# Four pieces instead of five for a far block's copy, and layer 1's key gather moved ahead of layer 0's value stores

## The chip, the cores and the metric

The kernel runs on one core of one Trainium2 chip. The metric is the device time of one execution in microseconds (us); the median of three runs of the kernel before is 405.74 us (405.36 to 406.79).

## The reference, cut to what matters

A trunk of two layers is run for a prompt (256 positions) and for 8 samples with one new position each. A layer normalises x, multiplies it with one combined input matrix, runs three groups side by side (a causal convolution of width 31, trailing means, and a dilated attention), and multiplies the concatenated results with an output matrix. What matters here are the samples' caches of keys and values, 2048 positions of 6 heads of 64 per sample and layer:

```python
kk = jnp.concatenate([k_buf, k], axis=1)
vv = jnp.concatenate([v_buf, v], axis=1)
o = dilated_attention(q, kk, vv, k_buf.shape[1])
yc = o.reshape(B, T, C_ATT) * jax.nn.silu(c_gate)
n_keep = min(MAX_WINDOW, kk.shape[1])
new_k = kk[:, -n_keep:]
new_v = vv[:, -n_keep:]
y = jnp.einsum('bte,ed->btd', jnp.concatenate([ya, yb, yc], axis=-1), w_out)
```

So each cache (2 layers, keys and values, 8 samples, 2048 rows of 1536 B) comes out once more, shifted by one row, and the attention of a sample reads only a part of its rows: the last 128 (near), every 4th of the 384 before them (mid), and every 16th of the first 1536 (far).

## The kernel before, in words

All arithmetic is float32, 128 partitions wide. TensorE (PE) carries the projections: 25 tiles of input weights per layer (`proj`, L586, 8 matmuls of 128x264 each) and 8 of output weights (`wout`, L723). Weights come in loads of three tiles (1536 KB) through a ring of three buffers `wt`; ScalarE (ACT) issues the next load when it has taken a buffer's last tile (`load_behind`). VectorE (DVE) runs the convolution's taps and the samples' scores. The order of all of this is one hand-written list, `SCHEDULE`, which every compute engine walks. Neither the list nor any instruction of PE, DVE or ACT is touched by the change.

The caches are moved in two ways.

- **The copies (GpSimd, POOL, L504).** Rows that the attention does not read go straight from the input cache to the output in DRAM. `COPIES` lists 48 transfers per layer: for keys and values and each of 8 samples two far halves (48 blocks of 16 rows, of which 15 are copied) and one mid part (96 blocks of 4 rows, of which 3 are copied). `max_dma_last_dim` caps a piece at `PIECE_ROWS` = 3 rows, 4608 B. So a far block is five pieces and a mid block one. POOL issues all 96 transfers in a row, layer 1's first, and waits for nothing but room in its queue.
- **The rows that are read (SyncE, SP).** `gather` loads near, mid and far rows into `kt` (keys) or `vt` (values), 20 slots per partition, 8 transfers for each of the three spans; `put_back` (L411, L416) stores the same tile into the output, shifted by one row. `kt` and `vt` are single buffers, so a layer's gather waits until the layer before has been read and stored.

SP issues all of these in one stream of program order, with waits on semaphores in between. Per layer: gather keys, gather values, store keys, states (the small state loads of the next layer and state copies of this one), store values. PE needs a layer's gathered values at step `spv` (L657), where it waits for all 24 transfers at once:

```python
pe.wait_ge(S["v_in"], nth(l, "v_in", per["v_in"]))
for j in range(a, b):
    v = vt[:, j, :] if j < NEW else kvb[:, 1, :]
    nc.tensor.matmul(psc[0:NH * NS, 0:C_ATT], spm[...], v, start=(j == 0), stop=(j == SLOTS))
```

DVE needs the keys at `sscore` (L1081), span by span. A value gather of layer 1 waits, span by span, until the stores of that span of layer 0 have landed (`v_near_out`, `v_mid_out`, `v_far_out`); a key gather does so with `k_near_out` and so on. At the end, ACT and DVE copy the turned output into `y_tok` (the memory of `kt`), SP issues its five stores (L477 to L485), and waits for everything.

Of the kernel before, what the change touches and what calls it, by code (L numbers as in the profile page):

```python
# [26 lines left out]
DEPTH, D_MODEL, SEQ, NS, PAST = 2, 1024, 256, 8, 2048  # L27
C_CONV, C_POOL, C_ATT, HD = 384, 256, 384, 64
# [17 lines left out]
GATHER = []  # L46
# [119 lines left out]
assert set(TABLE_BEFORE) <= set(SCHEDULE)  # L166
ACT_SCHEDULE = [_s for _s in SCHEDULE if _s != "ln2"]
ACT_SCHEDULE.insert(ACT_SCHEDULE.index(("proj", PIDX[("b_gate", 0)])), "ln2")
PIECE_ROWS = 3
GATHER_ROWS = 2  # L170
COPIES = [(kind, s, a, b, d) for kind in "kv" for s in range(NS) for a, b, d in
          ((0, GATHER[1][0] // 2, GATHER[2][1]), (GATHER[1][0] // 2, GATHER[1][0], GATHER[2][1]),
# [1 line left out]
SPANS = ("near", "mid", "far")  # L174
IN_FLIGHT = 16
# [4 lines left out]
def sample_rows(s):  # L180

    first = 2 * PER_S * (s // 2) + s % 2
    return slice(first, first + 2 * PER_S - 1, 2)
# [67 lines left out]
def trunk_program(nc, ins, const, const_at, outs):  # L251
    (y_prompt, y_sample, o_conv_p, o_pool_p, o_k_p, o_v_p, o_conv_s, o_pool_s, o_k_s, o_v_s) = outs
    with ExitStack() as ctx:
# [6 lines left out]
        def sem(name):  # L260
            return ctx.enter_context(nc.semaphore(name))
# [76 lines left out]
        per = {}  # L338

        S = {}  # L340
# [23 lines left out]
        copy_out = [sem(f"copy_out{i}") for i in range(IN_FLIGHT)]  # L364
# [11 lines left out]
        def nth(l, name, n):  # L376

            return l * per[name] + n + first.get(name, 0)
# [8 lines left out]
        def _(sp):  # L387
            def one(name, l):
                return ins[name][bass.ds(l, 1)]

            def gather(kind, l, g, name):

                tile = {"k": kt, "v": vt}[kind]
                (lo, d, n), at = GATHER[g], SPAN_AT[g]
                for s in SAMPLE_ORDER:
                    rows = one(f"cache_{kind}_win", l)[:, s, lo:lo + d * n * PER_S]
                    rows = rows.rearrange("o (a b e) h d -> (o a) b e (h d)", a=PER_S, e=d)[:, :, 0, :]
                    sp.dma_start(tile[sample_rows(s), at:at + n, :], rows, max_dma_last_dim=GATHER_ROWS * C_ATT * 4).then_inc(S[name], 16)  # L398

            def put_back(kind, l, g):  # L400

                name = f"{kind}_{SPANS[g]}_out"
                tile = {"k": kt, "v": vt}[kind]
                out = {"k": o_k_s, "v": o_v_s}[kind][bass.ds(l, 1)]
                (lo, d, n), at = GATHER[g], SPAN_AT[g]
                skip = 1 if lo == 0 else 0
                for s in SAMPLE_ORDER:
                    r = sample_rows(s)
                    rows = out[:, s, lo - 1 + d * n * skip:lo - 1 + d * n * PER_S]
                    rows = rows.rearrange("o (a b e) h d -> (o a) b e (h d)", b=n, e=d)[:, :, 0, :]  # L410
                    sp.dma_start(rows, tile[r.start + 2 * skip:r.stop:2, at:at + n, :]).then_inc(S[name], 16)  # L411
                if skip:
                    for r in range(2):
                        rows = out[:, r:NS:2, d - 1:d * n - 1]
                        rows = rows.rearrange("o s (b e) h d -> (o s) b e (h d)", e=d)[:, :, 0, :]
                        sp.dma_start(rows, tile[r:P:2 * PER_S, at + 1:at + n, :]).then_inc(S[name], 16)  # L416

            def states(l):
                if l > 0:
                    sp.wait_ge(S["tr_full"], nth(l - 1, "tr_full", TR["st1"] + 1))  # L420
                sp.dma_start(st_conv[:, :, :], one("state_conv", l).rearrange("o (r s) w c -> (o s w) r c", r=2)
                             ).then_inc(S["st_in"], 16)
                sp.dma_start(st_pool[:, :], one("state_pool", l).rearrange("o s w c -> (o s w) c")).then_inc(S["st_in"], 16)  # L423

            def keep_states(l):
                for name, out, keep in (("state_conv", o_conv_s, TAIL - 1), ("state_pool", o_pool_s, POOL_BUF - 1)):
                    sp.dma_start(out[bass.ds(l, 1), :, 0:keep].rearrange("o s w c -> (o s) (w c)").rearrange("s (e x) -> e s x", e=16),  # L427
                                 one(name, l)[:, :, 1:keep + 1].rearrange("o s w c -> (o s) (w c)").rearrange("s (e x) -> e s x", e=16))\
                        .then_inc(S["state_out"], 16)
# [8 lines left out]
            sp.dma_start(cst[:, early:], const[:, early:]).then_inc(const_in, 16)  # L438
            states(0)

            for l in range(DEPTH):
                if l == 0:
                    sp.wait_ge(S["pj_full"], nth(l, "pj_full", PIDX[("a_glu", 0)] + 1))
                if l > 0:
                    sp.wait_ge(S["ks_used"], nth(l - 1, "ks_used", len(SCORE_CUTS)))
                for g, span in enumerate(SPANS):
                    if l > 0:
                        sp.wait_ge(S[f"k_{span}_out"], nth(l - 1, f"k_{span}_out", per[f"k_{span}_out"]))
                    gather("k", l, g, f"k_{span}_in")

                if l == 0:
                    sp.wait_ge(x_copied, XROUNDS)
                    sp.wait_ge(S["pj_full"], nth(l, "pj_full", PIDX[("k", AT - 1)] + 1))
                else:
                    sp.wait_ge(S["sc_full"], nth(l - 1, "sc_full", NH + 1))
                for g, span in enumerate(SPANS):
                    if l > 0:
                        sp.wait_ge(S[f"v_{span}_out"], nth(l - 1, f"v_{span}_out", per[f"v_{span}_out"]))
                    gather("v", l, g, "v_in")

                if l == DEPTH - 1:
                    sp.wait_ge(S["pj_full"], nth(l, "pj_full", PIDX[("c_gate", AT - 1)] + 1))
                for g, span in enumerate(SPANS):
                    sp.wait_ge(S[f"k_{span}_in"], nth(l, f"k_{span}_in", per[f"k_{span}_in"]))
                    put_back("k", l, g)
                if l < DEPTH - 1:
                    states(l + 1)
                keep_states(l)

                if l == DEPTH - 1:  # L470
                    sp.wait_ge(S["sc_full"], nth(l, "sc_full", NH + 1))
                sp.wait_ge(S["v_in"], nth(l, "v_in", per["v_in"]))
                for g in range(len(SPANS)):
                    put_back("v", l, g)
# [17 lines left out]
        @block.gpsimd  # L492
        def _(pool):
            for name in START:
                pool.sem_inc(S[name], 1)

            pool.wait_ge(x_in, 32)
            for l in reversed(range(DEPTH)):
                for i, (kind, s, a, b, d) in enumerate(COPIES):
                    n = (DEPTH - 1 - l) * len(COPIES) + i  # L500
                    cache, out = (ins["cache_k_win"], o_k_s) if kind == "k" else (ins["cache_v_win"], o_v_s)
                    dst = out[l, s, a:b].rearrange("(c e f) h d -> c e (f h d)", c=16, f=d)[:, :, 0:(d - 1) * C_ATT]
                    src = cache[l, s, a:b].rearrange("(c e f) h d -> c e (f h d)", c=16, f=d)[:, :, C_ATT:d * C_ATT]
                    pool.dma_start(dst, src, max_dma_last_dim=PIECE_ROWS * C_ATT * 4).then_inc(copy_out[n % IN_FLIGHT], 16)  # L504

        @block.tensor
        def _(pe):
# [234 lines left out]
        def _(act):  # L742
# [18 lines left out]
            for l in range(DEPTH):  # L761
# [13 lines left out]
                for step in ACT_SCHEDULE:  # L775
# [121 lines left out]
                    elif kind in ("conv_p", "conv_s", "pool_ps"):  # L897
# [5 lines left out]
                        for dst, src, _, _ in copies:  # L903
                            last = A(dst[:, :], src, ACT.Copy, scale=0.5 if kind in ("conv_p", "conv_s") else 1.0)
                        last.then_inc(S["tr_free"], 1)
                        act.wait_ge(S["tr_free"], nth(l, "tr_free", TR[step] + 1))
                        for dst, _, out, row in copies:
                            o = out[bass.ds(l, 1)].rearrange("l b w c -> (l b w) c") if row is None else \
                                out[bass.ds(l, 1), :, row].rearrange("l s c -> (l s) c")
                            act.dma_start(o, dst[:, :]).then_inc(S["tail_out"], 16)  # L910
# [338 lines left out]
```

## Time and profile before

| what | value |
|---|---|
| median of 3 runs | 405.74 us |
| the profiled execution's own time | 407.23 us |
| its span, first to last instruction | 405.4 us |
| PE busy | 342.6 us (85%) |
| DVE busy | 231.9 us (57%) |
| DMA, moved over the span | 158.20 MB, mean 390 GB/s |
| DMA packets | 50,569 |
| mean granted clock of PE | 0.952 |

How to read it: a row of the profile's groups names line, engine, operation, tiles and count. "SPq", "ACTq" and "POOLq" are the engines as issuers of transfers; the queues that carry them are q1 for SP, q10 for ACT and q0 for POOL. A queue's row gives its packets, their bytes, and the time that they took as a share of 16 DMA engines over the stretch. A packet of 4 B closes a transfer on each engine and counts as a packet. A bracket behind a timeline row gives the idle time before it and what ended it.

### The profile page before, as it was taken

What the parts mean: (1) busy time and instruction counts of PE and PEld (TensorE: products, weight loads), DVE (VectorE), ACT (ScalarE), POOL (GpSimd) and SP (SyncE); (2) the same over time, 40 slices, a digit from 0 to 9 for tenths busy, and PEclk for the clock granted to TensorE, in tenths of its full rate; (3) what the DMA queues carried; (4) which work ended last, traced back from release to release, by engine and by line L of the source; (5) the groups of instructions that cost most, each with busy time, mean ns of one, the idle gap of its engine ahead of it and who ended that gap; (6) DMA issues with size and microseconds to landing.
All of it is one profiled execution on the core that took longest, in us unless ns stands there. A gap on an engine that the chain in (4) does not pass through costs nothing.

```text
span 405.4 us, 4582 instructions
## 1 busy us (share of the span) xinstructions
PE 342.6 (85%) x1534; PEld 265.4 (65%) x1534; DVE 231.9 (57%) x518; ACT 99.3 (24%) x234; POOL 56.5 (14%) x100
## 2 busy tenths in 40 slices
PE   3899999974899699899799999972989699899900
PEld 2688888852677465788588888852667555588800
DVE  2526998898769744310425898897857973311100
ACT  3201144311623423010200225321434324101010
POOL 3802022020220202202022020210201202000000
PEclk9999999997899999999899999998699999999965
DMA  8999999999999999999999999999999999999993
GB/s 291 415 419 415 417 415 411 413 385 404 409 386 399 415 360 365 416 365 417 418 412 395 418 418 414 416 410 417 405 389 373 415 391 338 411 391 386 349 374 154
DMA packets 50569, 158.20 MB, mean 390 GB/s; under 512 B 5400, under 2 KB 19938, under 8 KB 50034
## 3 DMA queue, kind: packets, MB, share of 16 engines
q0 software_dynamic: 19968, 84.94, 53.2%
q1 hardware_dynamic: 20812, 38.16, 25.6%
q10 hardware_dynamic: 9766, 34.82, 21.4%
q8 instruction: 12, 0.20, 0.2%
q14 instruction: 11, 0.09, 0.1%
HBM read 139.35 MB, written 104.42 MB: 601 GB/s over the span
## 4 chain that ended last, share of the span: by engine, by line
SPq 53%; PE 29%; DMA 8%; issue 2%; ACT 1%; DVE 1%; ACTq 0%; DVEq 0%
SPq L398 29%; SPq L411 20%; PE pj L586 15%; DMA vt<-in_cache_v_win 7%; PE pj L723 7%; PE psc L657 3%; SPq L427 2%; DMA vt<-in_x_sample 1%; SPq L423 1%; PE ptr L509 1%; SPq L416 1%; ACT hT L753 1%; PE prt L598 0%; PE ps L596 0%; PE ps L707 0%
## 5 line engine op out<-in xcount | busy, mean ns | idle before, releaser
L586 PE MATMUL pj<-hT,wt 128*128 128x264 f32 x800 | 191.2, 397 | 3.4 <-DVE hT L996 3.4
L586 PEld LDWEIGHTS pj<-hT,wt 128*128 128x128 f32 x800 | 154.5, 196 | 33.6 <-issue 7.3
L1141 DVE SCALAR_TENSOR_TENSOR yc<-u_ext,cst,yc 128x256 f32<-128x256 f32 x180 | 76.2, 480 | 2.8 <-DVE u_smp L1024 0.6
L723 PE MATMUL pj<-mix,wt 128*128 128x264 f32 x256 | 59.5, 387 | 0.0
L723 PEld LDWEIGHTS pj<-mix,wt 128*128 128x128 f32 x256 | 48.0, 190 | 8.0
L504 POOL DMA_DIRECT2D out<-in_cache_v_win x48 | 28.1, 591 | 162.5 <-issue 162.5
L504 POOL DMA_DIRECT2D out<-in_cache_k_win x48 | 28.2, 594 | 130.8 <-issue 124.2
L1211 DVE TENSOR_TENSOR xT<-xT,pj 128x264 f32<-128x264 f32 x16 | 6.9, 429 | 53.2 <-PE pj L723 53.2
L657 PE MATMUL psc<-vt,spm 128*48 128x384 f32 x80 | 26.9, 488 | 0.7 <-DMA vt<-in_cache_v_win 0.7
L822 ACT ACTIVATE ex<-pj 128x264 f32<-128x264 f32 x22 | 8.6, 391 | 76.8 <-PE pj L586 62.4
L509 PE MATMUL ptr<-cst,sc 128*128 128x128 f32 x36 | 7.1, 310 | 17.8 <-DVE sc L1057 17.8
L657 PEld LDWEIGHTS psc<-vt,spm 128*48 128x48 f32 x80 | 9.4, 123 | 15.5 <-issue 15.4
L1081 DVE TENSOR_TENSOR tok<-kt,qb 128x1536 f32<-128x1536 f32 x10 | 17.6, 1758 | 3.0 <-DMA kt<-in_cache_k_win 2.4
L509 PEld LDWEIGHTS ptr<-cst,sc 128*128 128x128 f32 x36 | 4.4, 153 | 21.6 <-DVE sc L1057 21.2
L1031 DVE SCALAR_TENSOR_TENSOR mix<-ex,pj 128x264 f32<-128x264 f32 x16 | 6.9, 428 | 19.9 <-ACT ex L822 19.6
L1084 DVE TENSOR_REDUCE ssc<-tok 128x24 f32<-128x1536 f32 x10 | 17.5, 1753 | 0.3
L1022 DVE SCALAR_TENSOR_TENSOR u_ext<-ex,pj 128x256 f32<-128x256 f32 x6 | 2.5, 422 | 23.4 <-ACT ex L822 23.4
L778 ACT ACT_TABLE_LOAD x12 | 15.4, 1283 | 0.4
L929 ACT ACTIVATE hT<-xT 128x264 f32<-128x264 f32 x8 | 3.4, 422 | 33.2 <-DVE xT L1211 33.2
L805 ACT ACTIVATE sqg<-pj 128x264 f32<-128x264 f32 x12 | 4.7, 392 | 26.9 <-PE pj L586 24.2
L881 ACT ACTIVATE sc<-sc,nmax 128x128 f32<-128x128 f32 x12 | 4.8, 402 | 25.0 <-DVE nmax L1050 19.4
L624 PE MATMUL psc<-qk 64*128 64x128 f32 x24 | 6.4, 352 | 5.1 <-DVE qk L1011 5.1
(165 smaller groups left out, 314.2 us busy)
## 6 DMA issues: line engine op xcount, KB each, us to landing
out<-in_cache_k_win POOLq DMA_DIRECT2D x32, 1080.0 KB, 70.1
out<-in_cache_v_win POOLq DMA_DIRECT2D x32, 1080.0 KB, 68.3
wt<-in_w ACTq DMA_DIRECT2D x21, 1536.0 KB, 14.8
out<-in_cache_k_win POOLq DMA_DIRECT2D x16, 432.0 KB, 66.6
out<-in_cache_v_win POOLq DMA_DIRECT2D x16, 432.0 KB, 69.5
kt<-in_cache_k_win SPq DMA_DIRECT2D x32, 144.0 KB, 25.3
vt<-in_cache_v_win SPq DMA_DIRECT2D x32, 144.0 KB, 22.7
kt<-in_cache_k_win SPq DMA_DIRECT2D x16, 192.0 KB, 17.1
```

Source lines behind the costliest of these rows:

```text
L398: sp.dma_start(tile[sample_rows(s), at:at + n, :], rows, max_dma_last_dim=GATHER_ROWS * C_ATT * 4).then_inc(S[name], 16)
L411: sp.dma_start(rows, tile[r.start + 2 * skip:r.stop:2, at:at + n, :]).then_inc(S[name], 16)
L504: pool.dma_start(dst, src, max_dma_last_dim=PIECE_ROWS * C_ATT * 4).then_inc(copy_out[n % IN_FLIGHT], 16)
L509: return nc.tensor.transpose(out, in_, C["ident"][0:rows, 0:rows])
L586: last = nc.tensor.matmul(pj[n % RING][:, 0:T], w[:, k * P:(k + 1) * P], hT[:, k, :], start=(k == 0), stop=(k == KD - 1))
L657: nc.tensor.matmul(psc[0:NH * NS, 0:C_ATT], spm[:, j * NH:(j + 1) * NH, :].rearrange("p h s -> p (h s)"), v, start=(j == 0), stop=(j == SL ...
L723: last = nc.tensor.matmul(pj[n % RING][:, 0:T], w[:, k * P:(k + 1) * P], mix[:, k, :], start=(k == 0), stop=(k == KD - 1))
L778: nc.scalar.preload_act_table_set(TABLE_BEFORE[step])
L822: A(ex[:, e % 2, :], src, ACT.Tanh, scale=0.5).then_inc(S["sig_ok"], 1)
L1081: V.tensor_tensor(tok4[:, :, :], kt[:, a:b, :], qb[:, None, :].to_broadcast([P, b - a, C_ATT]), ALU.mult).then_inc(S["kprod_ok"], 1)
L1084: last = V.tensor_reduce(ssc[:, a:b, :], tok4[:, :, :].rearrange("p j (h d) -> p j h d", h=NH), AX.X, ALU.add)
L1141: last = V.scalar_tensor_tensor(out=yc[:, t, 0:SEQ], in0=x_w, scalar=par[:, ROW_CW + w * CT + t:ROW_CW + w * CT + t + 1], in1=yc[:, t, 0:S ...
```

## The change

`PIECE_ROWS` gives way to `PIECES = 4`: the cap on a piece becomes 15 rows / 4 = 5760 B (3.75 rows). A far block's 23040 B go in four pieces instead of five; a mid block's 4608 B stay one piece. On SP, the gather of layer 1's keys is issued behind layer 0's state copies and ahead of layer 0's value stores, where it was behind them. No transfer is added or removed.

```diff
-PIECE_ROWS = 3
+PIECES = 4
...
-            for l in range(DEPTH):
+            def gather_keys(l):
                 if l == 0:
                     sp.wait_ge(S["pj_full"], nth(l, "pj_full", PIDX[("a_glu", 0)] + 1))
                 if l > 0:
...
+            gather_keys(0)
+            for l in range(DEPTH):
                 if l == 0:
                     sp.wait_ge(x_copied, XROUNDS)
                     sp.wait_ge(S["pj_full"], nth(l, "pj_full", PIDX[("k", AT - 1)] + 1))
                 else:
                     sp.wait_ge(S["sc_full"], nth(l - 1, "sc_full", NH + 1))
...
                 if l < DEPTH - 1:
                     states(l + 1)
                 keep_states(l)
+                if l < DEPTH - 1:
+                    gather_keys(l + 1)
 
                 if l == DEPTH - 1:
                     sp.wait_ge(S["sc_full"], nth(l, "sc_full", NH + 1))
...
-                    pool.dma_start(dst, src, max_dma_last_dim=PIECE_ROWS * C_ATT * 4).then_inc(copy_out[n % IN_FLIGHT], 16)
+                    pool.dma_start(dst, src, max_dma_last_dim=(GATHER[2][1] - 1) * C_ATT * 4 // PIECES).then_inc(copy_out[n % IN_FLIGHT], 16)
```

SP's stream between the two layers, as a difference (+ is the kernel after; names are destination<-source, `vt` and `kt` the tiles, "x8" eight transfers in a row):

```order
 L427 DMA out<-in_state_conv 16x8x696
 L427 DMA out<-in_state_pool 16x8x224
+L398 DMA kt<-in_cache_k_win 16x4x768 x8
+L398 DMA kt<-in_cache_k_win 16x6x384 x16
 L411 DMA out<-vt 16x3072 x8
 L411 DMA out<-vt 96x1x384 x8
 L411 DMA out<-vt 90x1x384 x8
 L416 DMA out<-vt 4x5x384 x2
-L398 DMA kt<-in_cache_k_win 16x4x768 x8
-L398 DMA kt<-in_cache_k_win 16x6x384 x16
 L398 DMA vt<-in_cache_v_win 16x4x768 x8
 L398 DMA vt<-in_cache_v_win 16x6x384 x16
```

The 24 key loads and the 26 value stores have changed places; the 24 value loads of layer 1 stand behind the same transfers as before.

POOL's stream at its start, before:

```order
L504 DMA out<-in_cache_k_win 48x5x1152 x2
L504 DMA out<-in_cache_k_win 96x1152
```

and after the change:

```order
L516 DMA out<-in_cache_k_win 48x4x1440 x2
L516 DMA out<-in_cache_k_win 96x1152
```

The two far halves go from 48 x 5 pieces of 1152 elements to 48 x 4 pieces of 1440; the mid part is as it was. This pattern repeats for all 32 pairs of halves.

## Rows read from the trace of the kernel before

**Rows 1.** The page's first line: the span.
```profile
span 405.4 us, 4582 instructions
```

**Rows 2.** The page's table of DMA queues over the whole span.
```profile
q0 software_dynamic: 19968, 84.94, 53.2%
q1 hardware_dynamic: 20812, 38.16, 25.6%
q10 hardware_dynamic: 9766, 34.82, 21.4%
```

**Rows 3.** Windows: busy us (x instructions) per engine, granted clock, DMA share, GB/s.
```profile
76.00:327.00 251.00, 218.91 (x987) 168.75 (x985) 165.32 (x353) 68.28 (x176) 35.09 (x60) 0.96 1.03 401
...
395.00:405.00 10.00, 0.00 (x0) 0.00 (x0) 0.00 (x0) 0.00 (x0) 0.00 (x0) 0.50 0.42 166
```

**Rows 4.** The chain that ended last, around layer 1's values: start us, us, what.
```profile
298.17 29.32 DMA vt<-in_cache_v_win
```

**Rows 5.** PE's timeline there, in layer 1.
```profile
327.62 5.33 PE L657 MATMUL psc<-vt,spm 128*48 128x384 f32 x16 [0.71 <-DMA vt<-in_cache_v_win]
```

**Rows 6.** SP's timeline of transfers issued from 76 us on.
```profile
76.13 29.38 SPq L398 DMA_DIRECT2D vt<-in_cache_v_win  x24
105.55 39.22 SPq L411 DMA_DIRECT2D out<-kt  x24
...
160.43 44.13 SPq L411 DMA_DIRECT2D out<-vt  x24
...
206.00 50.75 SPq L398 DMA_DIRECT2D kt<-in_cache_k_win  x24
256.85 44.20 SPq L398 DMA_DIRECT2D vt<-in_cache_v_win  x24
```

**Rows 7.** DMA queues in the window 76:327.
```profile
q0 software_dynamic: 12874, 54.75, 55.1%
q1 hardware_dynamic: 12520, 22.16, 23.9%
q10 hardware_dynamic: 6768, 23.60, 23.5%
```

**Rows 8.** DMA queues in the window 126:132.
```profile
q1 hardware_dynamic: 183, 1.01, 40.3%
q0 software_dynamic: 181, 0.76, 31.2%
q10 hardware_dynamic: 180, 0.74, 30.2%
```

**Rows 9.** DMA queues in the window 24:76.
```profile
q1 hardware_dynamic: 2249, 3.70, 19.0%
```

**Rows 10.** PE's timeline around a stall in layer 1.
```profile
272.82 3.83 PE L586 MATMUL pj<-hT,wt 128*128 128x264 f32 x16
284.75 0.90 PE L509 MATMUL ptr<-cst,sc 128*128 128x128 f32 x3 [8.10 <-DVE sc L1057]
...
287.86 5.65 PE L586 MATMUL pj<-hT,wt 128*128 128x264 f32 x16
```

**Rows 11.** Timeline of the end: PE's last matmul, the last copy, the last store issued.
```profile
385.09 0.27 PE L509 MATMUL ptr<-cst,xT 128*8 128x128 f32 x1
...
385.88 0.57 ACT L941 COPY kt<-ptr 8x512 f32<-8x512 f32 x1
...
393.69 0.40 SPq L485 DMA_DIRECT2D out<-kt  x1
```

**Rows 12.** DMA issues: transfers, KB each, median us from issue to landing.
```profile
out<-vt SPq DMA_DIRECT2D x16, 144.0 KB, 23.7
cst<-in_const SPq DMA_DIRECT2D x1, 72.5 KB, 1.9
```

**Rows 13.** DVE's timeline: the wait for layer 1's far keys.
```profile
280.37 1.76 DVE L1081 TENSOR_TENSOR tok<-kt,qb 128x1536 f32<-128x1536 f32 x1 [2.44 <-DMA kt<-in_cache_k_win]
```

**Rows 14.** SP's own waits.
```profile
SPq L487 <- DMA out<-in_cache_v_win: 8.6, 2, 7.1
```

More of the change, by code:

```diff
@@ L449, in _, with gather_values, keys_back @@
                     gather("k", l, g, f"k_{span}_in")
+            def gather_values(l, g):
+                span = SPANS[g]
+                if l > 0:
+                    sp.wait_ge(S[f"v_{span}_out"], nth(l - 1, f"v_{span}_out", per[f"v_{span}_out"]))
+                gather("v", l, g, "v_in")
+            def keys_back(l, g):
+                span = SPANS[g]
+                sp.wait_ge(S[f"k_{span}_in"], nth(l, f"k_{span}_in", per[f"k_{span}_in"]))
+                put_back("k", l, g)
+            gather_keys(0)
+            for l in range(DEPTH):
                 if l == 0:
@@ L455, in _ @@
                     sp.wait_ge(S["sc_full"], nth(l - 1, "sc_full", NH + 1))
[L456 to L459, printed above, removed]
+                for g in range(len(SPANS)):
+                    gather_values(l, g)
                 if l == DEPTH - 1:
                     sp.wait_ge(S["pj_full"], nth(l, "pj_full", PIDX[("c_gate", AT - 1)] + 1))
-                for g, span in enumerate(SPANS):
-                    sp.wait_ge(S[f"k_{span}_in"], nth(l, f"k_{span}_in", per[f"k_{span}_in"]))
-                    put_back("k", l, g)
+                for g in range(len(SPANS)):
+                    keys_back(l, g)
                 if l < DEPTH - 1:
```

## Prediction
> **What bounds the kernel now.** I read the queue table and the windows first, then the chain of waits, then the timelines of SP and PE. What a measurement of this kernel can tell from no change is about 0.3%, or 1.2 us.
>
> The DMA engines are full: over 76 to 327 us their share is 1.03 (packets overlap a little), and only the last ten microseconds fall to 0.42 [rows 3]. SP waits 8.6 us at the very end for the copies [rows 14]. So the kernel looks like one that ends when its bytes are through. But a second thing ends at the same time. The chain of waits goes from SP's last value load of layer 1, issued at 298.17 and landed 29.32 us later, to PE's step `spv` [rows 4], where PE had been idle for 0.71 us for just this landing [rows 5]. From there PE runs almost without a gap to its last matmul at 385.1 to 385.4 [rows 11], and the output's stores follow. So the landing of layer 1's values at 327.5 has no slack at all towards PE's end.
>
> What sets that landing? SP is never out of work from 76 us on: its issues stand end to end in the timeline, 24 loads taking 44 to 51 us where the queue is full and 29 where it starts empty [rows 6]. And the queue's pace shows in the packet counts. From 76 to 327 q0 (the copies) took 12,874 packets and q1 (SP) 12,520 [rows 7]. In 126 to 132, where SP stores near rows in large packets, the three queues took 181, 183 and 180 packets, though q1 moved 1.01 MB and q0 0.76 [rows 8]. So the engines serve the queues in turns, one packet each whatever its size, and SP moves one packet per copy packet. **How long a copy packet takes is a part of SP's pace.**
>
> **The change part by part.**
>
> *A packet's cost.* Share times 16 engines times 405.4 us [rows 1], over the packets [rows 2]: q0 172.8 ns at 4254 B on average, q1 79.8 ns at 1834 B, q10 142.1 ns at 3566 B. Between q0 and q1 that is 38.4 ns per 1000 B and 9.3 ns per packet; between q1 and q10, 36.0 and 13.8.
>
> *Fewer packets.* 64 far transfers x 48 blocks are 3072 blocks, each one piece less. 3072 x 9.3 ns / 16 engines = 1.8 us less DMA work (2.6 by the other pair; nothing as the lower bound). This is a gain only if the bytes set the end.
>
> *Longer turns.* q0 keeps 84.94 MB in 19,968 - 3072 = 16,896 packets: 5027 B on average, 773 B more. A turn of q0 takes 773 x 0.0384 = 29.7 ns more, 28.8 ns of wall time at a share of 1.03 (27 to 31 by the other pair, or by plain proportion). From 76 to 327 SP's queue needs 12,520 / 16 = 782 turns: 782 x 28.8 ns = **22.5 us** later. From 24 to 76 it needs 2249 / 16 = 141 [rows 9]: 4.0 us, which carry over only as far as the key loads are still queued when SP issues the value loads at 76. Bounds 0 and 4, and I take 3, since those loads are the last transfers in that queue. Layer 1's values land 25.5 us later, at 353.0. Bounds: 16 if a third of it is caught up by a hole in the weight queue or by cheaper store phases, 29 if all prices stand at their upper end.
>
> *The moved key gather.* 24 loads go ahead of 26 stores on SP. Both are ahead of the value loads before and after, so the number of turns up to the values does not change: cost nothing. What it buys: far keys now come just in time, DVE waits 2.44 us for them [rows 13]. With the longer turns and the old place they would come some 20 us late; in the new place they are issued from about 160 plus 9 us on [rows 6] and land tens of microseconds before their use. So the move hides what the pieces would cost the keys, and takes away the 2.44 us, but PE waits for the values anyway, so neither shows. The cover is that wait: without it the gain would be up to 2.4 us.
>
> *New waits.* Key loads must see layer 0's key stores landed; the last of them are issued by 146 us [rows 6], 14 us before the first load and over 40 before the far ones: nothing. Value loads must see layer 0's value stores landed, now right ahead of them. From the last far store to the first far load lie 16 loads, 16/24 x 44.2 = 29 us [rows 6], more at the new pace, against a median landing of 23.7 us [rows 12]: nothing, with an upper bound in the rivals. Weight loads: 24 turns per engine each, +0.7 us; no wait for weights shows in PE's rows, so nothing.
>
> *After the stall.* PE now stands still for 25 us. After a stall of 8.10 us the same 16 matmuls took 5.65 us at the lower clock instead of 3.83, and the transposes 0.90 [rows 10]. I take 2.5 us, bounds 1.8 and 4.
>
> *The end.* PE's last matmul moves from 385.4 to 385.4 + 25.5 + 2.5 = 413.4. Before, its stores took until 405.4, since they stood behind SP's queue: the last was issued at 393.69 though its data were ready at 386.5 [rows 11]. After, the copies are through (they gain what SP loses), and the stores meet an empty queue: about 1.1 us for the copies out of PSUM, issue, 1.08 MB at 401 GB/s [rows 3] (2.7 us), and 1.9 us for a small transfer's landing [rows 12], together 6 (bounds 5 and 8). So 14 of the 28 us are swallowed by the tail, and SP's final wait for the copies is gone. Sum: 413.4 + 6 = 419.4 us of span against 405.4, +14.0. The profiled execution took 407.23 us, 1.8 above its span, and the median of the runs is 405.74; on that median, 419.7.
>
> **The rivals.**
>
> 1. *The bytes set the end (faster).* If q0's longer pieces did not slow q1, for instance because the engines hand out bytes and not packets, the values would stay at 327.5 and 1.8 us of work would go: 403.9. For it: share 1.03, and SP's last wait for copies. Against it: the counts of rows 8, where a packet mix of other sizes left the turns equal. It decides if q1's packets before 327 stay at 12,520. The Trainium skill, "DMA: Bandwidth & Descriptors", section "Why small descriptors are slow (HBM only)", gives a fixed overhead to each packet, which is the reason for this case; the 9.3 ns of rows 2 agree in kind. Chance 0.11.
> 2. *The same, but the pieces cost extra at their ends.* 5760 B are 22.5 times 256 B, so every second piece starts halfway between two multiples of 256 B. If such a piece costs 128 B of extra fetch at both ends, a block costs 256 B more: 3072 x 256 B x 0.0384 ns / 16 = 1.9 us, which eats the 1.8: 405.8, no change. The rows have no price for it. The Trainium skill, same page, section "How a descriptor splits into AXI transactions", says that a transaction must start on a 256 B boundary and bytes before the start still cost beats. Chance 0.04.
> 3. *A smaller delay.* The break-even is a value landing 11.5 us late (385.4 + 11.5 + 2.5 + 6 = 405.4). If SP caught up to 14 us, the span would be 407.9, the time 408.2. It would need turns in which q0 has nothing; POOL keeps its queue full, so little speaks for it. Chance 0.08.
> 4. *The value stores land late.* If a far store takes 35 us to land in the new place, the far loads wait some 5 us more: 424.7. Chance 0.06.
> 5. *The cap does nothing*, because pieces are cut again on the way to the engines: 405.7. The order shows 48x4x1440, so 0.03.
>
> **How the numbers follow.** The forecast, 419.7, has 0.68; its own range from the bounds is 412 to 425. Slower by over 0.3% are the forecast, 3 and 4: 0.82; no change are 2 and 5: 0.07; faster is 1: 0.11. The range leaves out rivals 1, 2 and 5 and the edges of the others: 409 to 426.
>
> **What would show it.** After: 16,896 packets in q0; the wait of PE at `spv` for `vt` grows from 0.71 to some 26 us; the landing moves to about 353; q0 and q1 still count alike up to there; q0's packets end 20 us before the span does; no wait of DVE for `kt`; SP no longer waits for copies at the end. The prediction is wrong if that landing is before 339, or if the store of the output still takes 20 us behind a PE that ends at 413.

## The result

The changed kernel is **slower**: 423.57 us median (421.69 to 424.89, 4 runs) against 406.06 us (405.36 to 406.79, 4 runs). The ratio is 1.042, interval 1.039 to 1.045. The forecast was 419.7 us, in the range of 409 to 426. Its profiled execution took 421.69 us, with a span of 419.9 us; the sum had said 419.4. That execution was the shortest of four. So the sum hit its span to 0.5 us and missed the median by 3.9. That the span was hit so closely is in part luck: three terms of the sum were off, and they made up for each other, as the part on the prediction shows.

### The profile page after: what moved, and what is told of

Read it like the earlier page. It is cut to its first block, busy times and chain, and to the rows that moved or that the text cites. A ratio compares the mean times of both kernels' runs of the same rounds, so it can differ in the third digit from the quotient of the medians.

```text
span 419.9 us, 4582 instructions
## 1 busy us (share of the span) xinstructions
PE 345.8 (82%) x1534; PEld 266.2 (63%) x1534; DVE 231.8 (55%) x518; ACT 99.2 (24%) x234; POOL 53.8 (13%) x100
## 3 DMA queue, kind: packets, MB, share of 16 engines
q0 software_dynamic: 16896, 84.94, 51.0%
## 4 chain that ended last, share of the span: by engine, by line
SPq 59%; PE 29%; DMA 8%; issue 2%; ACT 1%; DVE 1%; ACTq 0%; DVEq 0%
SPq L398 34%; SPq L411 21%; PE pj L598 15%; PE pj L735 7%; DMA vt<-in_cache_v_win 6%; PE psc L669 4%; SPq L423 1%; DMA vt<-in_x_sample 1%; SPq L427 1%; PE ptr L521 1%; SPq L416 1%; SPq L421 1%; ACT hT L765 1%; PE prt L610 0%; PE ps L608 0%
## 5 line engine op out<-in xcount | busy, mean ns | idle before, releaser
L598 PE MATMUL pj<-hT,wt 128*128 128x264 f32 x800 | 188.9, 394 | 3.4 <-DVE hT L1008 3.4
L669 PE MATMUL psc<-vt,spm 128*48 128x384 f32 x80 | 29.5, 524 | 30.0 <-DMA vt<-in_cache_v_win 30.0
L516 POOL DMA_DIRECT2D out<-in_cache_v_win x48 | 26.8, 565 | 156.7 <-issue 156.7
L516 POOL DMA_DIRECT2D out<-in_cache_k_win x48 | 26.9, 567 | 109.7 <-issue 102.9
L776 ACT ACTIVATE r_h<-ps,cst 128x264 f32<-128x264 f32 x4 | 1.9, 480 | 53.6 <-PE ps L719 50.2
```

The lines of the kernel that those rows point to most:

```text
L516: pool.dma_start(dst, src, max_dma_last_dim=(GATHER[2][1] - 1) * C_ATT * 4 // PIECES).then_inc(copy_out[n % IN_FLIGHT], 16)
L598: last = nc.tensor.matmul(pj[n % RING][:, 0:T], w[:, k * P:(k + 1) * P], hT[:, k, :], start=(k == 0), stop=(k == KD - 1))
L669: nc.tensor.matmul(psc[0:NH * NS, 0:C_ATT], spm[:, j * NH:(j + 1) * NH, :].rearrange("p h s -> p (h s)"), v, start=(j == 0), stop=(j == SL ...
```

## The profile after

The page's head and its queue table, after the change (columns: packets, MB, share of 16 engines). They answer to [rows 1, 2].

```profile
span 419.9 us, 4582 instructions
DMA packets 47497, 158.20 MB, mean 377 GB/s; under 512 B 5400, under 2 KB 19938, under 8 KB 46962
q0 software_dynamic: 16896, 84.94, 51.0%
q1 hardware_dynamic: 20812, 38.16, 25.3%
```

q0 carries the same bytes in the forecast 16,896 packets. The trace's own list of packets gives their sizes: 12,288 of 5760 B (the far pieces), 3072 of 4608 B (the mid ones) and 1536 of 4 B. q0's share gives 0.510 x 16 x 419.9 us / 16,896 = 202.8 ns per packet, where the forecast was 172.8 + 29.7 = 202.5 ns. The bytes and the packets of q1 are untouched.

The DMA queues of the changed kernel in the windows 76:327 and 24:76. They answer to [rows 7, 9].

```profile
q0 software_dynamic: 11363, 57.16, 57.2%
q10 hardware_dynamic: 6908, 23.82, 23.7%
q1 hardware_dynamic: 11224, 19.51, 21.3%
...
q1 hardware_dynamic: 1949, 3.30, 17.3%
```

q0 and q1 still take the same number of packets, but both took fewer: by 327 us SP's queue is 12,520 - 11,224 = 1296 packets behind, 81 on each engine. What q0 loses in packets it gains in bytes (57.16 MB against 54.75), and q1 pays (19.51 against 22.16).

The chain that ended last (start us, us, what), then PE's timeline there. They answer to [rows 4, 5].

```profile
329.16 26.60 DMA vt<-in_cache_v_win
355.76 0.14 issue
```
```profile
355.89 7.28 PE L669 MATMUL psc<-vt,spm 128*48 128x384 f32 x16 [30.00 <-DMA vt<-in_cache_v_win]
363.11 3.83 PE L598 MATMUL pj<-hT,wt 128*128 128x264 f32 x16
```

The values of layer 1 land at 355.76 instead of 327.49, 28.3 us later. PE's wait for them grows from 0.71 to 30.00 us, and the 16 matmuls behind it take 7.28 us instead of 5.33: 1.95 us for the lower clock. The windows of the stall after the change and of the same step before it show this clock (busy us per engine, granted clock, DMA share, GB/s):

```profile
327.00:356.00 29.00, 0.10 (x1) 0.14 (x2) 5.22 (x17) 0.29 (x1) 0.00 (x0) 0.54 1.02 378
```
```profile
327.00:351.00 24.00, 23.38 (x87) 12.73 (x88) 11.02 (x28) 7.85 (x11) 2.89 (x5) 1.00 1.03 371
```

PE stood still for 30 us, and its granted clock was 0.54 on average there, nearly all of it at the lower of the two levels (1.2 GHz). It was still 0.50 over the first 3 us of the matmuls and 1.00 (2.4 GHz) from 363 us on. From there PE's rows are those of before, shifted.

SP's timeline from 76 us on, for [rows 6].

```profile
76.09 36.09 SPq L398 DMA_DIRECT2D vt<-in_cache_v_win  x24
112.23 43.44 SPq L411 DMA_DIRECT2D out<-kt  x24
...
170.86 57.24 SPq L398 DMA_DIRECT2D kt<-in_cache_k_win  x24
228.15 48.67 SPq L411 DMA_DIRECT2D out<-vt  x24
276.86 1.83 SPq L416 DMA_DIRECT2D out<-vt  x2
278.79 52.58 SPq L398 DMA_DIRECT2D vt<-in_cache_v_win  x24
```

The loss is not in one place. The first value loads take 36 us to issue instead of 29; layer 0's state copies end at 171 instead of 160; the last value loads are issued from 279 instead of 257. Every stretch is longer.

SP's own waits at the end, and the last PE and output rows, for [rows 11, 14].

```profile
SPq L493 <- ACT kt L952: 11.5, 1, 11.5
SPq L489 <- ACT kt L949: 3.0, 1, 3.0
SPq L502 <- DMA out<-kt: 1.1, 1, 1.1
```
```profile
415.32 0.27 PE L521 MATMUL ptr<-cst,xT 128*8 128x128 f32 x1
```

SP's longest wait at the end is now for PE's output as ACT copies it, 11.5 us, and no longer for the copies. The copies are through by 389 us, 31 us ahead of the end, where the forecast had said 20. The queues of the window 389:420:

```profile
q1 hardware_dynamic: 2563, 4.20, 40.4%
q8 instruction: 1, 0.02, 0.2%
```

q0 has no row there. PE ends at 415.6 and the span 4.3 us later, where before 20 us lay between.

## The experiments

The kernel before took 405.6 us beside the first four runs (order only to six pieces, in the order they are told) and 409.9 to 410.8 us beside the others, so times are compared by their ratio to the kernel before of the same group, and spans of the two groups only with that 1% in mind. The change itself was measured beside the first group only. "Wait" is PE's wait for the values in layer 1.

| kernel | q0 packets | wait, us | span, us | ratio (interval) |
|---|---|---|---|---|
| order only | 19,968 | none | 404.5 | 1.0015 (0.998 to 1.005) |
| pieces only | 16,896 | 2.1 | 421.0 | 1.037 (1.033 to 1.041) |
| the change | 16,896 | 30.0 | 419.9 | 1.042 (1.039 to 1.045) |
| three pieces | 13,824 | 30.3 | 440.2 | 1.086 (1.081 to 1.091) |
| six pieces | 13,824 | 25.1 | 437.9 | 1.083 (1.080 to 1.087) |
| ten pieces | 19,968 | none | 408.6 | 1.003 (1.000 to 1.005) |
| fifteen pieces | 19,968 | 0.4 | 410.9 | 1.0005 (0.997 to 1.004) |
| first half large | 18,432 | 15.9 | 406.7 | 0.9975 (0.995 to 1.000) |
| second half large | 18,432 | 20.1 | 411.1 | 1.002 (1.000 to 1.004) |
| states behind | 16,896 | 26.6 | 416.2 | 1.0275 (1.023 to 1.033) |
| first half large, states behind | 18,432 | 10.7 | 407.2 | 1.000 (0.997 to 1.002) |
| first quarter large, states behind | 19,200 | 5.7 | 409.2 | 1.001 (0.998 to 1.003) |
| late large | 19,200 | 1.0 | 410.6 | 1.001 (0.999 to 1.004) |

### Each part of the change alone

```diff
 # order_only, against the changed kernel
-PIECES = 4
+PIECES = 5
 # pieces_only, against the kernel before
-PIECE_ROWS = 3
+PIECES = 4
-pool.dma_start(dst, src, max_dma_last_dim=PIECE_ROWS * C_ATT * 4)
+pool.dma_start(dst, src, max_dma_last_dim=(GATHER[2][1] - 1) * C_ATT * 4 // PIECES)
```

> Layer 1's keys ahead of layer 0's value stores, pieces as before (five of 4608 B). Theory (a copy piece's length sets SP's pace): no turn of SP ahead of the values is added or removed, so layer 1's values land at 327 +- 2 us, the wait of PE for them stays under 2 us, span 405.4, ratio to before 0.997 to 1.003. The wait of DVE for the keys (2.44 us) is gone. Rival (the new order brings the loss, by value stores that land late ahead of the value loads): the values land 5 us or more later and the ratio is 1.01 or more.

Measured 1.0015: no change. The queue rows of its window 76:327 count 12,855 and 12,569 packets, as before, and the wait of DVE for the keys is gone. The prediction's rival of late value stores falls with it, as far as the order alone can bring it.

> Four pieces of 5760 B, order as before. Theory: the values land at 355 +- 3 us as in the changed kernel, because the same packets of SP stand ahead of them; the far keys land some 25 us later than before, at about 305, so DVE waits some 25 us for them, which the wait for the values mostly covers. Span 420 to 425, ratio 1.035 to 1.05. Rival (the order brings the loss): ratio under 1.01. Rival (the order is worth much here): ratio 1.06 or more.

Measured 1.037. The pieces alone bring the loss, and the new order changes little of it. How it is split is another matter. DVE's timeline of the run with the pieces alone, keys in the old place:

```profile
273.76 1.76 DVE L1081 TENSOR_TENSOR tok<-kt,qb 128x1536 f32<-128x1536 f32 x1 [13.45 <-DMA kt<-in_cache_k_win]
...
289.76 1.76 DVE L1081 TENSOR_TENSOR tok<-kt,qb 128x1536 f32<-128x1536 f32 x1 [3.00 <-DMA kt<-in_cache_k_win]
...
308.33 1.76 DVE L1081 TENSOR_TENSOR tok<-kt,qb 128x1536 f32<-128x1536 f32 x1 [12.60 <-DMA kt<-in_cache_k_win]
```
```profile
357.30 7.02 PE L657 MATMUL psc<-vt,spm 128*48 128x384 f32 x16 [2.07 <-DMA vt<-in_cache_v_win]
```

DVE waits 29.1 us in three pieces for the keys, and PE, which needs DVE's results, then only 2.07 us for the values: both start `spv` within 1.4 us of each other. So the move of the key gather is what the prediction said: it hides the keys' delay behind the values' delay, and no gain or loss can be told: 1.037 and 1.042 differ by 0.5%, and their intervals overlap. The keys' far span was put at 305 and landed at 308.3.

### Longer and shorter turns

```diff
 # three_pieces and six_pieces, against the changed kernel
-PIECES = 4
+PIECES = 3      # six_pieces: 6, and the cap of a mid part stays 4608 B
```

> The changed kernel with three pieces of 7680 B (7680 instead of 5760). Packets in q0: 13,824, 6144 B on average, a turn 72.6 ns longer than before at 38.4 ns per 1000 B. Until the copies run out, that would be 782 x 70 ns = 55 us for the values; but POOL's copies then end before the values are in (13,824 / 16 = 864 turns), after which SP has the engines to itself, so the delay is 40 to 50 us, landing at 367 to 378, span 432 to 442, ratio 1.065 to 1.09. Rival (bytes, not packets, are shared out, and the loss of 5760 B is one of this size alone, such as its odd multiple of 128 B; 7680 is 30 x 256): ratio 1.00 or below.

Measured 1.086, span 440.2, values at 376.0: inside the expected ranges. Its q0 row is the check on the price: 0.481 x 16 x 440.2 us / 13,824 = 245.1 ns a packet, where 9.3 ns and 38.4 ns per 1000 B make 245.2.

```profile
q0 software_dynamic: 13824, 84.94, 48.1%
...
376.12 7.38 PE L669 MATMUL psc<-vt,spm 128*48 128x384 f32 x16 [30.32 <-DMA vt<-in_cache_v_win]
```

PE also waits for the values of layer 0 here, 12.2 us, which the expectation had not listed.

> The changed kernel with six pieces of 3840 B (mid parts stay 4608 B). Packets in q0: 23,040, 3687 B on average, a turn 21.8 ns shorter than before. Theory: the values land 17 to 22 us earlier than before, at 305 to 310, PE no longer waits for them, its last matmul is at 384 to 385; the copies now end last: 3072 more packets x 9.3 ns / 16 = 1.8 us of work, and q0's last packet comes 4 to 7 us later than before. Span 405 to 409, ratio 1.00 to 1.01. Rival (fewer, longer packets are better for the engines as such, so shorter ones lose time everywhere): ratio over 1.015. Rival (PE's wait for the values is what holds the time before, too): ratio under 0.997.

Measured 1.083, the opposite of what the theory expected. Of the three cases only the rival "ratio over 1.015" has room for it, and its reason, shorter packets that lose time everywhere, does not hold, since the packets did not get shorter. The queue tables say why. This is the run with six pieces of 3840 B:

```profile
q0 software_dynamic: 13824, 84.94, 48.3%
q1 hardware_dynamic: 20812, 38.16, 25.3%
...
374.24 7.01 PE L669 MATMUL psc<-vt,spm 128*48 128x384 f32 x16 [25.14 <-DMA vt<-in_cache_v_win]
```

23,040 packets were expected; there are 13,824, the count of three pieces. The packets are longer than the pieces: the trace's list of packets has 9216 of 7680 B in q0 and none of 3840 B, as with three pieces. Two pieces went out as one packet, and the time is that of three pieces. The theory stood (turns by packet), the assumption that a piece is a packet did not. Two more runs tell what joins pieces.

```diff
 # ten_pieces and fifteen_pieces, against the changed kernel; n counts POOL's copies
-max_dma_last_dim=(GATHER[2][1] - 1) * C_ATT * 4 // PIECES
+max_dma_last_dim=C_ATT * 12 if d == 4 else (GATHER[2][1] - 1) * C_ATT * 4 // (10)    # or (15)
```

> The changed kernel with ten pieces of 2304 B per far block. The run with six pieces of 3840 B had 13,824 packets in q0, as many as the one with three of 7680 B, and the same time: the queue joined two pieces into a packet of 7680 B. New theory: GpSimd's queue closes a packet when it holds 4096 B or more (4608, 5760 and 7680 B pieces stand alone, two of 3840 B join), and the packet is SP's turn. Then two pieces of 2304 B join to 4608 B: q0 has 19,968 packets as before, the values land at 327 +- 4 us and the ratio is 0.995 to 1.01. Rival (two neighbours always join from six pieces on, at any size, or only pieces that end up over 4096 B by one join are special): other counts, such as 35,328 packets (no joining), values 30 us or more earlier, and 3072 x 5 x 9.3 ns / 16 = 8.9 us more work, ratio 1.015 to 1.03. Rival (the piece, not the packet, is the turn): the same as this.

> The changed kernel with fifteen pieces of 1536 B per far block. Pieces of 3840 and 2304 B were joined in pairs. If GpSimd's queue closes a packet at 4096 B or more, three pieces of 1536 B join (3072 B is not enough): 4608 B, 19,968 packets in q0, PE waits under 6 us for the values, ratio 0.99 to 1.015. If neighbours join in pairs, whatever their size: packets of 3072 B, at least 15 / 2 per block, some 27,600 to 29,200 in q0; SP's turns are then shorter than before by 50 ns, PE does not wait for the values, and the DMA work is 4 to 6 us more, ratio 1.01 to 1.03.

```profile
q0 software_dynamic: 19968, 84.94, 53.4%
```
```profile
q0 software_dynamic: 19968, 84.94, 53.0%
```

The first row is the run with ten pieces, the second with fifteen. Both have the packets of five pieces (18,432 of 4608 B in the trace's list, none of 2304 or 1536 B), a wait for the values of 0 and 0.4 us, and the time of the kernel before. So 2 x 2304 B and 3 x 1536 B both became 4608 B: a packet stays open at 3840 B or less and is closed at 4608 B or more. The 4096 B of the theory lie between; these runs don't place the limit closer. The Trainium skill, "DMA: Bandwidth & Descriptors", section "SWDGE vs HWDGE vs iDMA", calls a packet the boundary at which an engine switches context and puts it at 4096 B "preferably". The rows agree that the packet and not the single piece is the unit: with six pieces SP kept the pace of three. They also show that a packet can be larger than 4096 B, by its last piece.

### Where in the kernel the long packets stand

```diff
 # first_half_large (second_half_large: 5 if n < 48 else 4), against the changed kernel
-max_dma_last_dim=(GATHER[2][1] - 1) * C_ATT * 4 // PIECES
+max_dma_last_dim=C_ATT * 12 if d == 4 else (GATHER[2][1] - 1) * C_ATT * 4 // (4 if n < 48 else 5)
```

> The changed kernel with 5760 B pieces only in the first 48 of 96 copies (layer 1's), 4608 B in the rest. Theory: the delay of the values grows with the turns that SP takes beside large packets. The first 48 copies are served until about 200 us; SP has some 400 turns from 76 us to there, 400 x 28.8 ns = 11.5 us and the 3 us from the key loads: the values land 14 to 17 us late, at 341 to 345, PE waits 14 to 17 us, its last matmul is at 401 to 404, and the end comes 4 to 8 us behind it: span 406 to 411, ratio 1.002 to 1.017. Rival (the loss comes from the copies that run beside the last loads, around 280 to 330 us): landing at 328 +- 2, ratio 1.00. Rival (a fixed loss as soon as any piece is 5760 B): landing at 355, ratio 1.04.

The wait is 15.9 us and the landing at 342.8, as expected: half the long packets, about half the delay. PE ends 17 us later than before. But the ratio is 0.9975, under the expected 1.002 to 1.017. The windows of this run (busy us per engine, granted clock, DMA share, GB/s) show what the delay is traded for:

```profile
385.00:390.00 5.00, 5.00 (x27) 4.24 (x26) 0.75 (x2) 0.00 (x0) 0.00 (x0) 1.00 0.91 359
...
395.00:400.00 5.00, 5.00 (x25) 4.25 (x25) 0.43 (x1) 0.00 (x0) 0.00 (x0) 1.00 0.74 262
400.00:405.00 5.00, 2.18 (x12) 1.35 (x11) 1.12 (x2) 1.05 (x2) 0.00 (x0) 0.94 0.27 104
```

The DMA engines run dry while PE still works, and the output's stores then end 4.3 us behind PE instead of 20. PE's delay of 17 us is nearly all paid out of the tail. The ratio is also helped by its group: the kernel before took 409.9 us beside this run and not 405.6. The tail bound by the DMA engines had grown there, PE's own chain hardly (the matmuls of `spv` start at 328.1 with ten pieces in this group and at 326.8 with the order only in the first). Against the 405.4 us of the first group this run's span of 406.7 would be a ratio of about 1.003, inside the expected range; that is an estimate and was not run.

> The changed kernel with 5760 B pieces in the last 48 copies instead of the first 48. As many packets as with the first 48 large. Theory: the large packets now stand beside SP's turns from about 203 us to the end, some 400 turns before the values land, so PE's wait is 10 to 15 us, much as with the first half; but the value stores and the output's stores behind them also meet long turns, and the copies do not run out before them. Last packet of the copies at 393 to 398, span 407 to 413, ratio 1.005 to 1.020. Rival (only the number of packets counts): the time of the kernel with the first half large, ratio 0.995 to 1.00.

The wait is 20.1 us, over the 10 to 15 expected. The copies' last packets start after 400 us and not at 393 to 398. The span of 411.1 is inside its range, but the ratio of 1.002 (0.9995 to 1.0042) is below the expected one. It is slower than with the first half large, as the theory says, but a difference of 0.4% between two ratios is near what they can tell, so the rival that counts only packets is not excluded. Where in the kernel the long packets stand matters little for the time.

### The queue ahead of the values

```diff
 # states_behind, against the changed kernel
                 if l < DEPTH - 1:
                     states(l + 1)
-                keep_states(l)
                 if l < DEPTH - 1:
                     gather_keys(l + 1)
+                else:
+                    keep_states(l)
...
                 for g in range(len(SPANS)):
                     gather_values(l, g)
+                if l > 0:
+                    keep_states(l - 1)
```

> The changed kernel, with layer 0's two state copies (18 packets on each DMA engine) issued behind layer 1's value loads instead of ahead of them. Theory: 18 turns less ahead of the values; a turn takes 251 us / (11,224 / 16) = 0.358 us in the changed kernel, so the values land 6.4 us earlier (349.3), and the span falls by as much, to 413.5; ratio 1.022 to 1.032. Rival (the engines hand out bytes: the two copies are 460 KB, 1.1 us at 400 GB/s): 1 us earlier, ratio 1.037 to 1.045.

Measured 1.0275, interval 1.0225 to 1.0325: inside the expected ratio and outside the rival's 1.037 to 1.045. But two nearer comparisons give only half of the 6.4 us. PE's wait falls from 30.0 to 26.6 us and `spv` starts at 352.77 instead of 355.89, 3.1 us earlier; the medians are 423.57 and 420.43 us, also 3.1 apart. This run stands in the second group, in which the kernel before took 1% more, and the change was not run there. The ratios of the two groups, 1.0275 and 1.042, differ by 1.5% or 5.9 us, but a slower kernel before makes a ratio smaller by itself, so this may overstate the gain. Moving the two copies of 460 KB brought 3 to 6 us. That is more than their bytes explain (1.1 us); whether it is the whole 6.4 us of 18 turns these runs don't show.

### Versions that might beat both

```diff
 # all three with the edit of states_behind, and
-max_dma_last_dim=(GATHER[2][1] - 1) * C_ATT * 4 // PIECES
+max_dma_last_dim=C_ATT * 12 if d == 4 else (GATHER[2][1] - 1) * C_ATT * 4 // (5 if n < 72 else 4)    # late_large
+max_dma_last_dim=C_ATT * 12 if d == 4 else (GATHER[2][1] - 1) * C_ATT * 4 // (4 if n < 48 else 5)    # first_half_states
+max_dma_last_dim=C_ATT * 12 if d == 4 else (GATHER[2][1] - 1) * C_ATT * 4 // (4 if n < 24 else 5)    # first_quarter_states
```

> A version that might beat both: pieces of 4608 B in the first 72 copies and of 5760 B in the last 24, layer 1's keys ahead of layer 0's value stores, layer 0's state copies behind layer 1's value loads. Theory: PE no longer waits for the values (they land at 318 to 323 us against a need at 327), its last matmul comes 0.5 to 1 us earlier, and 16 x 48 = 768 packets fewer save 0.45 us of DMA work; the end is set by the DMA engines as before. Span 404 to 406, ratio 0.995 to 1.002. Rival (the values' landing is what holds the end of the kernel before): ratio under 0.99.

> Joins two edits that were run apart: 5760 B pieces in the first 48 copies only, and layer 0's state copies behind layer 1's value loads. With the first edit alone the values landed 15.9 us after PE's need, PE ended at 402.5 and the span was 406.7; the copies' last packet came at 396. Theory: the 18 turns bring the values 6 us earlier, PE ends at 396 to 397, its stores land 4 to 6 us later, and the DMA engines set a floor: their share was already under 1 from 385 us on, some 7 us idle in all, so the span is 401 to 403.5, ratio 0.985 to 0.994. Rival (the engines' bytes set the floor where it is): ratio 0.996 to 1.00.

> The same with 5760 B pieces in the first 24 copies only. Theory: the values are 7 to 9 us late by the pieces and 6 us early by the state copies: PE waits 2 to 5 us and ends at 388 to 391. SP's stream has fewer turns behind it than before, but the copies end at 399 to 400; the end is set by SP's stores and the copies together: span 402 to 405, ratio 0.990 to 0.999. Rival (PE's end plus 4 us sets the span): 393 to 396, ratio 0.97.

None beats the kernel before: 1.001, 1.000 and 1.001. In the first the ratio was in the expected range, but the values landed at 326.1 and not at 318 to 323, PE still waited 1.0 us, and its rival (under 0.99) fell. PE ended at 384, 26.6 us before the end of the span, and the last to land were SP's own stores. In the second the values did come earlier (a wait of 10.7 us instead of 15.9) and PE ended at 399, but the stores landed 7.9 us behind it and the span stayed at 407.2; the expected 0.985 to 0.994 failed, and the rival, a floor by the engines' work, held. The third was expected at 0.990 to 0.999 and shows the same floor: PE waited 5.7 us (2 to 5 expected) and ended 17 us before the span did. Its windows of the tail:

```profile
385.00:390.00 5.00, 5.00 (x26) 4.25 (x25) 0.43 (x1) 0.00 (x0) 0.00 (x0) 1.00 0.94 361
...
395.00:400.00 5.00, 0.00 (x0) 0.00 (x0) 0.00 (x0) 0.00 (x0) 0.00 (x0) 0.50 0.84 314
400.00:405.00 5.00, 0.00 (x0) 0.00 (x0) 0.00 (x0) 0.00 (x0) 0.00 (x0) 0.50 0.39 138
```

PE is done at 392 and the engines work on to 409, though not all of them: their share is 0.39 from 400 to 405 us. So with waits of 0, 5.7, 10.7, 15.9 and 20.1 us the ratio stays between 0.9975 and 1.003, and with 26.6 and 30.0 it is 1.0275 and 1.042. So there are two bounds. The DMA engines' work holds the kernel before, at 405.4 us. PE behind its values and 4.3 us of stores is the other; it stands at 385.4 + 4.3 = 389.7 us there, 15.7 us or 4% lower. A delay of the values can grow to some 14 us before it shows (the gap less the 1.95 us that the lower clock takes after a stall), and the change's 28.3 us lifted the lower bound over the upper one.

## Why the prediction was right, and where it was off

- **Two ends** (no slack from the values to PE's end, DMA share of 1.03): right, with one correction. The two do not end at the same time: PE ended 20 us before the kernel, and its stores need 4.3 us when the engines are free. The prediction's sum did count this slack ("14 of the 28 us are swallowed"). The runs with smaller delays show the DMA engines' end as a floor.
- **Fewer packets** (1.8 us less DMA work, no part of the sum): true of q0 alone. Its packets took 0.532 x 405.4 = 215.7 us per engine before and 0.510 x 419.9 = 214.1 after. But q1's same packets took 103.8 before and 106.2 after, so the engines' work as a whole did not fall.
- **Turns by packet, whatever its size**: right, by the counts of the changed kernel and by three pieces. What six pieces corrected is the unit: the packet, which may hold several pieces. At 4608 and 5760 B the two are the same, so the forecast did not suffer.
- **A packet's price** (38.4 ns per 1000 B and 9.3 ns): right, 202.8 ns against 202.5.
- **The length of SP's turns** (28.8 ns more each): too small while weights are loaded, and made up for afterwards. In the window 76:327 SP's queue took 12,520 / 16 = 782 turns in 251 us before, 0.321 us each, and 701 turns after, 0.358 us each: 37 ns more. The forecast lengthened only q0's share of a turn. The weight queue (q10) loads at PE's pace and not at SP's: it took 6908 packets in this window against 6768. Spread over fewer turns of SP these are 0.615 against 0.541 per turn, and at 142 ns each 10 ns more, by estimate; with q0's 29 ns this accounts for the 37. From 327 to 355 us the weight queue is silent (one packet), and 1535 packets or 96 turns took 28 us, 0.292 each. That the average over 76 to 355 us, 0.350 us, lies just 29 ns over the 0.321 of before is the balance of the two, which the forecast did not work out.
- **The carry-over from the key loads** (3 us taken, 0 to 4 as bounds): too small, and outside its bounds. By 76 us q1 had taken 1949 packets instead of 2249, 19 turns less, and at 0.33 us a turn these are 6.2 us of work that the value loads found ahead of them. The forecast had multiplied its 141 turns with 28.8 ns. Measured, a turn of this stretch took 0.427 us instead of 0.370, 57 ns more, again with more packets of the weight queue in each (1908 / 1949 against 1888 / 2249). With the 22.5 us forecast for the turns this makes 28.7; 28.3 were measured, and 25.5 forecast.
- **The clock after the stall** (2.5 us, bounds 1.8 and 4): 1.95.
- **The tail** (6 us, bounds 5 and 8): 4.3. The forecast counted the landing of all five stores behind PE's end; the stores of the output's first half were issued at 404 us, before PE was done. The tail was 1.7 us too long and the clock's term 0.55; together they nearly cancel the 2.8 us that the landing was late by. So 385.4 + 28.3 + 1.95 + 4.3 = 419.9 against 419.4 is a right mechanism and a lucky sum.
- **The median**: the forecast added the 0.34 us by which the median of before lay over the span of another execution. But an execution's time lies 1.8 us over its own span (407.23 and 405.4 before, 421.69 and 419.9 after), which makes 1.5 of the 3.9 us. The four runs of the changed kernel lie 421.7 to 424.9, over spans of 419.9 to 423.1, so the execution with the profile was the shortest. Where the other three spend up to 3 us more has no trace; their mean granted clock was 0.922 to 0.930 against 0.937.
- **The moved gather at nothing**: right, 1.0015 alone. DVE's 2.44 us went and did not show.
- **The prediction's own range of 412 to 425**: it does not follow from the terms' bounds, which add up to 385.4 + 16 + 1.8 + 5 = 408 and 385.4 + 29 + 4 + 8 = 426.
- **The rivals.** Bytes as the bound alone fell. Extra cost of pieces that start halfway between multiples of 256 B: none seen. 256 B more per block would be 3072 x 256 x 0.0384 / 16,896 = 1.8 ns on the mean packet, 204.3 ns; 202.8 were measured against 202.5 without it. With pieces of 7680 B, which are whole multiples of 256 B, the same line was right to 0.1 ns. But the mean packet of the other two runs with the same pieces is 201.7 (pieces only) and 202.2 ns (states behind), so 1.8 ns is not far above what two runs differ by. The Trainium skill ("DMA: Bandwidth & Descriptors", section "How a descriptor splits into AXI transactions") states the cost in beats of the bus; whether it is there and hidden these runs can't tell, and it shows in no time here. A smaller delay fell. Its break-even was put at 11.5 us; with the measured terms it is 405.4 - 385.4 - 1.95 - 4.3 = 13.8. The runs whose values landed 15.3 and 18.4 us late still show a ratio of 0.9975 and 1.002. Most of the rest is their group: the kernel before took 409.9 and 410.8 us there, a span of some 408 to 409 with 1.8 us taken off, so the break-even lies near 17 us, by estimate. Late value stores: not seen in the change; SP has no wait of that kind among its rows. The cap that does nothing fell with the count of 16,896.

## What to carry to other kernels

Where several queues share the DMA engines, count packets before bytes: a queue that is always full takes one turn for every packet of the others, and making its packets 25% longer slows a stream of small packets beside it, though the engines' total work hardly changes. Before making transfers of a background queue coarser, follow the stream that a compute engine waits for, count its packets up to the one that is waited for, and multiply by the extra length of the other queue's packet. If a third queue runs at a pace of its own, as the weights do here, each turn also takes in more of its packets, and the loss is larger. And where two bounds lie near each other, ask how far the lower one may rise before it shows: here it was some 14 us, and the change took 28.3.

## What the runs showed that was not expected

GpSimd's queue joins neighbouring pieces into one packet as long as it holds 3840 B or less: 3 x 1536, 2 x 2304 and 2 x 3840 B went out as 4608, 4608 and 7680 B. A smaller cap on the pieces can so make the packets longer: with six pieces of 3840 B the kernel took 8.3% more time than with five of 4608 B. The cost of issuing does not follow the packets. With the same packets of 4608 B a copy took POOL 592 ns on average with five pieces, 626 with ten and 689 with fifteen; with packets of 7680 B it took 580 with three pieces and 593 with six. Four pieces took 566, so the growth with the pieces is not steady at the low end. None of it shows in the time, which is that of the packets.
